# RWKV gate products of a hybrid trunk, spread over the lumps of the triangular inverse: a lump of 6 between the 64 level's two products, 2 left in the tail

## The reference

```python
p = h @ w_in                                    # RWKV | mLSTM | branch gates (2 x 1024 columns)
y_r = rwkv7_branch(p_r, ...) @ branch_w_rwkv    # 8 heads of 64
y_m = mlstm_branch(p_m, ...) @ branch_w_mlstm   # 4 heads of 128
g_r, g_m = split(sigmoid(p_g), 2)
return (g_r * y_r + g_m * y_m) @ w_out

def step(s, inp):                               # RWKV-7, for every token
    sa = einsum('bhvk,bhk->bhv', s, a_t)
    s = s * w_t + sa[..., None] * b_t + v_t[..., None] * k_t
    return s, einsum('bhvk,bhk->bhv', s, r_t)
```

## Time and profile before

| | us |
|---|---|
| median of 3 runs | 1408.33 |
| lowest and highest run | 1407.04, 1410.0 |
| the profiled execution | 1409.51 |
| its span | 1407.5 |
| mean granted clock of TensorE | 0.999 of full speed |

### The profile page before, as it was taken

One profiled execution on the slowest core, in us unless ns is written; L12 is line 12 of the kernel. 1 busy time (PEld: TensorE's weight loads), 2 busy tenths in 40 slices (PEclk: granted clock), 3 DMA queues, 4 the chain that ended last, 5 costly groups with the idle time before them and its releaser, 6 DMA issues.

```text
span 1407.5 us, 30467 instructions
## 1 busy us (share of the span) xinstructions
PE 1385.3 (98%) x13536; PEld 1304.2 (93%) x13536; DVE 1028.7 (73%) x1718; ACT 288.4 (20%) x556; POOL 67.6 (5%) x137
## 2 busy tenths in 40 slices
PE   7999999999999999999999999999999999999998
PEld 3999999888978999999999999988998889999998
DVE  5899889778524769897988886787873375856565
ACT  2211101452222031110031110034332302211101
POOL 5000000000000000100000000000000000000000
PEclk9999999999999999999999999999999999999999
DMA  9999785443423658888767886554433257456530
GB/s 347 325 328 326 284 316 172 141 141 106 113 71 122 236 183 269 278 303 291 246 211 254 275 280 237 167 133 151 140 90 96 65 192 251 144 188 209 195 136 30
DMA packets 214051, 283.10 MB, mean 201 GB/s; under 512 B 13289, under 2 KB 177505, under 8 KB 213921
## 3 DMA queue, kind: packets, MB, share of 16 engines
q1 hardware_dynamic: 194976, 211.11, 46.5%
q0 software_dynamic: 17952, 69.21, 14.0%
q10 hardware_dynamic: 992, 0.85, 0.2%
HBM read 280.10 MB, written 1.05 MB: 200 GB/s over the span
## 4 chain that ended last, share of the span: by engine, by line
PE 96%; DVE 2%; DMA 1%; issue 1%; ACT 0%; ACTq 0%; SPq 0%; DVEq 0%
PE ps L1833 94%; PE ps L1837 1%; DVE ada_acc L1045 1%; DMA ada_stage<-in_ada_w_dram 1%; DMA xn<-in_x_dram 0%; PE ps L2332 0%; DVE ada_turn L1051 0%; DVE ada_red L1052 0%; DVE arena L1274 0%; DVE arena L1277 0%; DVE arena L1275 0%; DVE hT L1818 0%; ACT xn L696 0%; ACT hT L696 0%; DVE x L1218 0%
## 5 line engine op out<-in xcount | busy, mean ns | idle before, releaser
L1833 PE MATMUL ps<-hT,ring 128*128 128x128 f32 (+2 forms) x2448 | 394.3, 318 | 3.4 <-issue 2.1
L1833 PEld LDWEIGHTS ps<-hT,ring 128*128 128x128 f32 (+1 forms) x2448 | 349.9, 190 | 37.7 <-issue 10.7
L1833 PE MATMUL ps<-y_both,arena 128*128 128x128 f32 x2304 | 266.6, 275 | 1.0 <-issue 1.0
L1833 PEld LDWEIGHTS ps<-y_both,arena 128*128 128x128 f32 x2304 | 261.8, 192 | 1.5 <-issue 1.5
L1833 PE MATMUL ps<-arena 32*32 32x32 f32 (+6 forms) x4368 | 203.1, 230 | 2.5 <-issue 2.4
L1833 PEld LDWEIGHTS ps<-arena 32*32 32x32 f32 (+3 forms) x4368 | 192.6, 138 | 11.9 <-issue 9.8
L1833 PE MATMUL ps<-arena,ring 128*128 128x128 f32 (+1 forms) x1312 | 186.5, 294 | 0.0
L1833 PEld LDWEIGHTS ps<-arena,ring 128*128 128x128 f32 x1312 | 171.3, 191 | 6.6
L1045 DVE SCALAR_TENSOR_TENSOR ada_acc<-ada_stage,cond,ada_acc 128x1024 f32<-128x1024 f32 (+1 forms) x119 | 149.0, 1252 | 5.6 <-DMA ada_stage<-in_ada_w_dram 1.6
L1833 PE MATMUL ps<-y_both,ring 128*128 128x128 f32 (+1 forms) x1024 | 150.8, 301 | 0.0
L1833 PEld LDWEIGHTS ps<-y_both,ring 128*128 128x128 f32 x1024 | 138.7, 192 | 6.5
(11 more groups left out here) (317 smaller groups left out, 1341.4 us busy)
## 6 DMA issues: line engine op xcount, KB each, us to landing
ring<-in_ffn_w_in_dram SPq DMA_DIRECT2D x86, 1024.0 KB, 7.7
ada_stage<-in_ada_w_dram POOLq DMA_DIRECT2D x66, 1024.0 KB, 5.7
ring<-in_ffn_w_out_dram SPq DMA_DIRECT2D x44, 1024.0 KB, 6.7
ring<-in_mix_w_in_dram SPq DMA_DIRECT2D x46, 512.0 KB, 5.2
ring<-in_mix_w_in_dram SPq DMA_DIRECT2D x12, 1024.0 KB, 5.7
ring<-in_mix_w_in_dram SPq DMA_DIRECT2D x6, 1536.0 KB, 6.4
ring<-in_mix_w_out_dram SPq DMA_DIRECT2D x8, 1024.0 KB, 5.0
arena<-in_ada_w_dram SPq DMA_DIRECT2D x6, 1024.0 KB, 13.6
```

The costliest lines, as they stand in the source:

```text
L1833: return nc.tensor.matmul(out_, lhsT, rhs, start=start, stop=stop, **kw)
```

## The change

The counts of 11 places change, the total of 96 stays, and a new place "g" with 6 products is put between "turned a" and "xo", on TensorE and in ScalarE's order:

```diff
-GATE_PLACES = (("num", 5), ("n", 8), ("a", 8), ("b", 8), ("c", 8), ("d", 8), ("e", 8), ("f", 9), ("h", 7),
-               ("i", 4), ("j", 5), ("k", 5), ("tail", 13))
+GATE_PLACES = (("num", 5), ("n", 9), ("a", 10), ("b", 9), ("c", 9), ("d", 8), ("e", 10), ("f", 8), ("g", 6), ("h", 6),
+               ("i", 4), ("j", 5), ("k", 5), ("tail", 2))
@@ scalar
                     act(az[:, 8 * g:8 * g + 8, 0:64], view(ps[:, g, :], 8, 64), ACT.Copy, "turned a" if g else None)
+                gates("g")
                 ac.wait_ge(*PE.at(l, "xo"))
```

## The result

The changed kernel takes 1414.6 us in the median; the kernel before took 1409.1 in runs beside it. The ratio is 1.0038, with a 95% interval of 1.0022 to 1.0054. The change makes the kernel slower by about 5.6 us. One of the six executions of the changed kernel ran at a granted clock of 0.85, took 1583.31 us and is left out of the ratio. The forecast was 1407.1 us with a range of 1403.2 to 1410.8, so both the sign and the range were wrong.

What follows compares the result with a forecast made beforehand. TensorE, busy 98% of the span, was taken to bound the kernel, running out of instructions at packet borders. Products, lump and tail 0, packets -1.3, rounded to -1.2: 1408.33 - 1.2 = 1407.1 us, range 1403.2 to 1410.8.

Steps and rivals of the forecast that it cites:

- products moved: Gate products, 96 per layer before and after: 11 products (4.75 us) leave the tail and stand earlier; cost 0 net.
- the lump: New lump g behind the turns of turned a, before xo: taken as 0, bounds -0.1 to +0.2 us a layer.
- the tail: VectorE's norm ahead of TensorE's turns: of 5.7 us slack 4.75 go, 0.9 us are left; cost 0.
- two of the signs: Signs of being right: layer 0's pause at x 32 is gone; pauses in both stretches sum to 4 to 8 us.
- SyncE's queue: Weight loads for gates 6, 7 and the mLSTM branch start 2 to 7 us earlier, none later; cost 0 for consumers.
- the proportion: Shortfall of product-free stretches to 4.1 us falls from 14.1 to 11.7 us, so 7.5 us of pauses become 6.2.
- packets -1.3: Pauses at instruction packet borders in both layers' stretches shrink: a gain of 1.3 us, the term said to decide.
- the bound of +6.4 us: Worst case at packet borders: four stretches of 2.2 us or less each filled to 5.4 us, 13.9 us instead of 7.5.
- rival B: New borders meet branch loads in gt-h-qt of layer 0 and turned b of layer 1: +3 to +5 us, 1411.8; chance 0.08.
- Rival D: Nothing moves: pauses hang on packet counts, not on what stands between borders; total stays 1408.3; chance 0.15, inside "same".
- A: Fuller lumps a, b, c, e end five of eight border pauses: -5.7 us, 1402.6; chance 0.28.
- C: TensorE waits before the tail's turns for VectorE's norm: 0.4 us a layer, 0.8 in all, 1408.0; chance of mattering 0.04.

Runs made afterwards that it cites:

- refitted version: Changed kernel with both branch loads held until TensorE's y and gate counts chosen so stretches between packet borders hold products or last over 3.7 us: 1402.7 us, ratio 0.9951.
- both loads late: Changed kernel with the second mLSTM load and first RWKV load held until TensorE's y is done: 1408.75 us, ratio 0.9997 to the kernel before.
- only the RWKV load late: Changed kernel with only the first RWKV branch load held until TensorE's y; the mLSTM load as in the changed kernel: 1409.5 us, ratio 1.0007.
- borders moved by 256: Changed kernel with 256 more semaphore instructions on TensorE in layer 0's first feed-forward, a whole packet: 1415.5 us, ratio 1.0042.
- refitted, borders moved by 64: Kernel with refitted gate counts and both branch loads late, plus 64 more semaphore instructions on TensorE in layer 0's first feed-forward: 1407.5 us, ratio 0.9981.

## Why the prediction was wrong

**Right.** That pauses at packet borders are what the placement of products moves in this stretch; that the products moved, the lump and the tail cost nothing (lump g lasts 2.68 us, forecast 2.6; the idle time of VectorE 1.65, forecast 1.6); that no semaphore would be waited for; that lumps a, b, c and e gain (2.8 us in the first part, more than the 1.3 net that I gave the whole); that gt-h-qt of layer 0 gets a new pause and g32's goes. The trace of before read by distances of 128 records gave all of this. Not right were two of the signs: a pause stays at the end of x 32 in layer 0 (0.91 us of idle time at 412.04), and the pauses sum to 9.7 us, not 4 to 8.

**The size of the miss.** The stretches were to gain 1.3 us and lost 5.5. Of these 6.8 us, the pauses are 3.5 (+2.2 us in place of -1.3) and the clock is 3.3, for which the sum had no term at all.

**Wrong, first step: "SyncE's queue ... Cost 0 for their consumers", and its tie to the borders.** I asked only whether the moved loads would land in time. I noted that the mLSTM load moves to the start of i, and that the first RWKV load waits for "qt", "which comes 4.75 us later", but not that in the kernel before the first held back the second in the queue, until all risky stretches were past. So in layer 1 the RWKV load went not later but 2.9 us earlier (1121.19 against 1124.07). With product 112 in i it runs alone, in the y lump of layer 1. That pause measures 3.76 us and went to 0.81 us of idle time when this load alone was held.

**Wrong, second step: the proportion.** The term "packets -1.3" priced every stretch against a flat 4.1 us. The fifteen crossings of the kernels before and changed that end in a pause fall into two groups: eight take 2.4 to 3.7 us, seven 4.5 to 5.8. In the long ones the packet started only with the last pieces of a load. The longest, 5.8 us (1122.26 to 1128.02, counted back 128 records), is beyond the 5.4 that I took for the longest. A load under way is not enough by itself, though: in two of the short ones of the kernel before the packet (410.54, 1067.33) moved in the midst of a load, 1.3 and 0.9 us behind the first of its data. I had the two kinds in the text ("long ones fit with weights under way") and averaged them; the bound of +6.4 us that I worked out held the result (+5.6), but I cut the range at 1410.8, for I gave rival B only 0.08.

**Rival B** had the right mechanism and half of its place. Its stretch in layer 0 paused by 2.27 us (priced at 3.2). For layer 1 it named the turned b, which paused by 0.91 us, and not the y lump. By its own terms, 3.2 + 3.9 - 2, it should have stood at +5.1 us, 1413.4, and not at 1411.8. And it lacks the clock: no step priced what the half clock behind the two long pauses costs, 3.3 us in the changed kernel.

**Rival D**, and the rule of the Trainium skill (Runtime: NRT & Kernel Launch, "Instruction fetch mechanics") that crossing a block is mostly hidden, are refuted for this stretch: moving the borders by 148 instructions moves the time by 5.2 us, moving them by the 256 that the page gives as a block by 0.9. Rivals A and C did not occur; the refitted version shows what A would have taken, a placement checked against every border.

**Open.** Which packets a load holds back and which go ahead of it is not shown; the profile has no mark of when a packet is asked for. Whether a held packet waits in a shared DMA ring behind the load's descriptors or only for bandwidth was not tried. Nor is it settled when the clock falls: it did behind idle times of 1.31 (both loads late), 2.06 and 3.55 us (changed), and did not behind 2.09 (only the RWKV load late), 2.37 (borders moved by 256, layer 0) and 2.52 us (refitted, borders moved by 64).

## What to carry to other kernels

Where hundreds of tiny matmuls stand in a row, TensorE can outrun its own instruction stream. Waits named "issue" that lie 128 matmul records (256 instructions) apart are the sign, and every 128 records should then hold some 4 us of work, or up to 5.8 where a large load runs at that time. Filler belongs there first, and as its effect depends on where the borders fall, any edit ahead of it on that engine means fitting it again. When filler also releases ring slots, moving it moves loads: ask not only whether they land in time but what else is on the DMA queues while they run.

## What the runs showed of the hardware that I had not expected

A single load of 1 MB under way kept a 16 KB instruction packet from moving until the load's last pieces, 4.5 us after the load's issue; other packets moved in the midst of a load. PE went on 2.3 to 2.6 us after the start of the packet that it stood for, in each of the seven pauses of the changed kernel. Behind the pauses of 2.3 and 3.8 us in that kernel the granted clock fell (0.58 over lump k) and gate records took 0.427 us in place of 0.216, which put 1.6 and 1.7 us on top of the pauses themselves. And 256 additional semaphore instructions in a stretch of larger matmuls were free.
